# Squares in tiles of their own, x loaded once, weight loads in another order: a two-layer streaming encoder on 8 cores

## The reference

```
xn   = rms_norm(x, norm_mix)                       # x * rsqrt(mean(x*x) + eps) * g
q, k, v, pin, gates = split(xn @ w_in)             # 512, 128, 128, 512, 2 x 1024
q, k = rms_norm per head
a    = sliding-window attention(q, k, v) with ALiBi and a sink logit in the denominator
pl   = (trailing means of pin over 2, 4, 8, 16 frames - pin) @ w_pool * pool_scale
mix  = sigmoid(gates_0) * (a @ w_br_attn) + sigmoid(gates_1) * (pl @ w_br_pool)
x    = x + mix @ w_out
h    = rms_norm(x, norm_ffn) @ w_up                # 1024 -> 2 x 2816
hc   = conv_b + causal depthwise conv of width 3 over h
x    = x + (gelu(hc_gate) * hc_val) @ w_down       # 2816 -> 1024
```

## Time and profile before

| what | value |
|---|---|
| runs | 3413.95, 3782.05 and 3413.5 us, median 3413.95 |
| the profiled execution | 3412.9 us, of which the span of core 2 is 3411.3 |
| spans of cores 0 to 7 | 3407.0, 3378.5, 3411.3, 3379.6, 3380.1, 3408.5, 3407.7, 3378.3 |
| busy: PE, DVE, ACT, POOL | 3300.8 (97%), 2138.6 (63%), 1563.4 (46%), 990.5 (29%) |
| chain that ended last | PE 89%, DMA 5%, DVE 2%, issue 2%, ACT 1% |
| DMA | 385.28 MB, mean 113 GB/s |
| layer 0 mixer, FFN; layer 1 mixer, FFN | 0 to about 800, to 1760, to 2490, to 3411 us |

### The profile page before, as it was taken

The page is one execution under the profiler, slowest core; times in us unless marked ns, Lnnn a source line. Parts: engine busy times, 40 slices in busy tenths (PEclk is TensorE's granted clock), DMA queues, the critical chain, the costliest instruction groups (busy, mean ns, idle before and its releaser), DMA issues.

```text
span 3411.3 us, 53613 instructions; the slowest of 8 cores (3378.3 to 3411.3 us)
## 1 busy us (share of the span) xinstructions
PE 3300.8 (97%) x17682; PEld 1613.6 (47%) x17835; DVE 2138.6 (63%) x3379; ACT 1563.4 (46%) x2417; POOL 990.5 (29%) x1057
## 2 busy tenths in 40 slices
PE   6899999999999999999988899999989999999999
PEld 3544444444444444444444444444445555555554
DVE  3555556646667766677645455656476666776666
ACT  3444444425444644455535344444254444554444
POOL 3233322114323433234333222221143222333222
PEclk8899999999999999999988999999999999999999
DMA  9356666456523344233562333332543221212211
GB/s 194 82 159 139 145 140 139 103 170 213 148 82 95 90 130 118 82 96 94 174 209 57 101 99 99 100 99 77 176 173 108 89 79 56 77 56 89 88 45 45
DMA packets 186640, 385.28 MB, mean 113 GB/s; under 512 B 31712, under 2 KB 110208, under 8 KB 179648
## 3 DMA queue, kind: packets, MB, share of 16 engines
q1 hardware_dynamic: 173296, 279.43, 26.3%
q0 software_dynamic: 6592, 56.79, 10.4%
q10 hardware_dynamic: 6480, 45.62, 3.8%
HBM read 369.01 MB, written 115.41 MB: 142 GB/s over the span
## 4 chain that ended last, share of the span: by engine, by line
PE 89%; DMA 5%; DVE 2%; issue 2%; ACT 1%; POOL 0%; SPq 0%; ACTq 0%; DVEq 0%; POOLq 0%
PE psb L615 89%; DMA xsl<-xT 2%; DMA xsl<-x 1%; DMA xst<-xT 1%; DVE xn L624 1%; ACT psb L618 0%; PE psb L1117 0%; DVE PT L621 0%; ACT srt L618 0%; DMA xm<-xsl 0%; DMA w_kv<-wun 0%; DMA x<-xsl 0%; ACT L618 0%; DVE xsl L624 0%; DMA xst<-x0p 0%
## 5 line engine op out<-in xcount | busy, mean ns | idle before, releaser
L615 PE MATMUL psb<-xn,w_up 128*128 128x482 bf16 (+3 forms) x6336 | 1264.0, 362 | 16.4 <-DVE xsl L624 16.4
L615 PEld LDWEIGHTS psb<-xn,w_up 128*128 128x128 bf16 x6336 | 620.4, 98 | 657.0 <-issue 24.7
L621 POOL TENSOR_TENSOR actT<-ug,uv 128x480 bf16<-128x480 f32 (+3 forms) x360 | 424.7, 1180 | 1135.6 <-ACT ug L618 987.5
L624 DVE SCALAR_TENSOR_TENSOR ug<-psb,pv,ug 128x480 f32<-128x480 f32 (+3 forms) x792 | 557.5, 704 | 125.7 <-ACT ug L618 42.5
L615 PE MATMUL psb<-actT,w_dn 128*128 128x480 bf16 (+3 forms) x3168 | 631.3, 361 | 0.0
L624 DVE SCALAR_TENSOR_TENSOR uv<-psb,pv,uv 128x480 f32<-128x480 f32 (+3 forms) x792 | 557.2, 703 | 51.9 <-ACT uv L618 4.6
L618 ACT ACTIVATE ug<-psb,pv 128x480 f32<-128x480 f32 (+3 forms) x396 | 291.9, 737 | 558.1 <-PE psb L615 545.1
L615 PE MATMUL psb<-xn,w_eg 128*128 128x512 bf16 x1970 | 473.5, 380 | 3.7 <-issue 0.3
L615 PEld LDWEIGHTS psb<-actT,w_dn 128*128 128x128 bf16 x3168 | 310.0, 98 | 315.5
L618 ACT ACTIVATE uv<-psb,pv 128x480 f32<-128x480 f32 (+3 forms) x396 | 292.7, 739 | 224.0 <-PE psb L615 223.4
L618 ACT ACTIVATE tg<-psb,hgb 128x512 f32<-128x512 f32 (+2 forms) x288 | 185.1, 649 | 306.9 <-PE psb L615 286.5
(11 more groups left out here) (165 smaller groups left out, 2685.6 us busy)
## 6 DMA issues: line engine op xcount, KB each, us to landing
xsl<-x SPq DMA_DIRECT2D x96, 512.0 KB, 4.8
xsl<-xT SPq DMA_DIRECT2D x88, 512.0 KB, 6.0
wb<-wun POOLq DMA_DIRECT2D x42, 1024.0 KB, 11.0
xm<-xsl SPq DMA_DIRECT2D x64, 512.0 KB, 5.2
xsl<-xm SPq DMA_DIRECT2D x56, 482.0 KB, 7.8
xsl<-xm SPq DMA_DIRECT2D x56, 460.0 KB, 4.4
w_up<-wb ACTq DMA_DIRECT2D x22, 1024.0 KB, 7.4
xsl<-xm SPq DMA_DIRECT2D x28, 480.0 KB, 4.9
```

What stands on the lines that cost most here:

```text
L615: S.op("pe", lambda e: e.matmul(out=out, lhsT=lhsT, rhs=rhs, start=start, stop=stop), reads=reads, writes=writes)
L621: S.op(eng, lambda e: e.tensor_tensor(out=out, in0=a, in1=b, op=op), reads=reads, writes=writes)
L624: S.op("dve", lambda e: e.scalar_tensor_tensor(out=out, in0=a, scalar=s, in1=b, op0=op0, op1=op1), reads=reads, writes=writes)
```

## The change

1. `sqx0` to `sqx2`, three tiles of [128, 512] fp32, take the squares, one block of 128 channels at a time. The sum runs in `sqx0` on POOL; the squares alternate between `sqx1` and `sqx2`. x stays in its slot until `scale`, and the second `loads()` goes, except for the norm of layer 1's third group (in `ffn_down` of layer 0's last group).
2. up6 to up10 move into the first FFN group, after pairs j = 0, 2, 4, 6, 8, and dn0 to dn5 follow after j = 10, 12, ..., 20.
3. Layer 1's small group has its residual in `resS`, loaded at the start of the layer.
4. For groups 1 and 2 of each layer the pooling difference reads `pinb` and not the bank, and the bank is given back before the window sums.
5. The second group's x at the start is loaded right behind `pv` and no longer waits for `w_kv`; `w_kv` no longer waits for `xst0_1`.
6. The planner: DMAs of different queues share the rate (280 bytes per ns), a 64-row matmul of 256 columns or more costs 0.76 of a full one and not 0.5.
7. The tile `spare` goes; `xst0` lies over `padE`, `resS`, `padF` and `mixT`.

```diff
-DMA_START, DMA_END, DMA_RATE = 1400, 600, 300.0
+DMA_START, DMA_END, DMA_RATE = 1400, 600, 280.0
...
-        return c / 2 if p.ins[0].shape[0] == 64 and n >= 256 else c
+        return c * 0.76 if p.ins[0].shape[0] == 64 and n >= 256 else c
...
+        def serve(queue, t, size):
+            t = max(t + DMA_START, busy.get(queue, 0.0))
+            ends = sorted(u for q, u in busy.items() if q != queue and u > t)
+            left = float(size)
+            while ends and t + left * (1 + len(ends)) / DMA_RATE > ends[0]:
+                left -= (ends[0] - t) * DMA_RATE / (1 + len(ends))
+                t = ends.pop(0)
+            busy[queue] = t + left * (1 + len(ends)) / DMA_RATE
+            return busy[queue] + DMA_END
...
+        sqx = [sb(f"sqx{i}", [128, 512], F32) for i in range(3)]
...
+        resS = su("m", "resS", [128, KT, 18], F32, rows("resS", 4, 144))
...
             def stat(self, p):
                 A, B = self.A, self.B
-                if self.keep is not None:
...
-                i = self.slot[p]
-                act(xs[i][:, :, A:B], xs[i][:, :, A:B], ACTF.Square, [f"xs{i}"], [f"xs{i}"])
-                if p > 0:
-                    a = self.acc
-                    tt("pool", xs[i][:, :, A:B], xs[a][:, :, A:B], xs[i][:, :, A:B], ALU.add, [f"xs{a}", f"xs{i}"], [f"xs{i}"])
-                self.acc = i
+                for h in range(2):
+                    k = 2 * p + h
+                    if self.keep is not None:
+                        X, xr, b = self.keep[0][:, k, A:B], f"{self.keep[1]}{p}", k % 3
+                    else:
+                        i = self.slot[p]
+                        X, xr, b = xs[i][:, h, A:B], f"xs{i}", 0 if k == 0 else 1 + k % 2
+                    if self.keep is not None and self.keep[2] is not None and h == 1:
+                        tt("dve", sqx[b][:, A:B], X, X, ALU.mult, [xr], [f"sqx{b}"])
+                    else:
+                        act(sqx[b][:, A:B], X, ACTF.Square, [xr], [f"sqx{b}"])
+                    if self.keep is None:
+                        if k > 0:
+                            tt("pool", sqx[0][:, A:B], sqx[0][:, A:B], sqx[b][:, A:B], ALU.add, ["sqx0", f"sqx{b}"], ["sqx0"])
+                        continue
+                    if k == 0:
+                        self.bk = PB.get()
+                    mm(psb[:, self.bk, A:B], onesf[:, :], sqx[b][:, A:B], k == 0, k == KT - 1, ["onesf", f"sqx{b}"], pr(self.bk))
...
+            if G.i < 3 and G.samp is None:
+                PB.put(bk)
             window(G, j, r, n, G.C0, bk, 0 if G.own else G.C0)
...
-            stt(G.eD[0][:, j, col + c0:col + n], cur[:, 16 + c0:16 + n], 1.0 / w, psb[:, bk, b0 + c0:b0 + n], ALU.mult, ALU.subtract,
-                [cr] + pr(bk), [dr])
+            stt(G.eD[0][:, j, col + c0:col + n], cur[:, 16 + c0:16 + n], 1.0 / w, pinb[r][:, 16 + c0:16 + n] if flat else psb[:, bk, b0 + c0:b0 + n], ALU.mult, ALU.subtract,
+                [cr] + ([f"pinb{r}"] if flat else pr(bk)), [dr])
...
+                    if own:
+                        stt(resS[:, 2 * p + hh, :], psb[:, bks[c], C0:N], 0.5, resS[:, 2 * p + hh, :], ALU.mult, ALU.add,
+                            pr(bks[c]) + [f"resS{p}"], [f"resS{p}"])
...
         nj0.loads()
         dma(pv[:], pvec, [], ["pv"], "c0")
+        nj1.loads()
...
-        load_first("kv", ["xst0_1"])
+        load_first("kv")
         load_first("pin")
         load_first("q")
-        for p in range(4):
-            nj1.load(p, ["w_kv"])
...
         nj2.stat_end()
-        nj2.loads()
...
                         if m == 5:
                             job.stat_end()
-                        if m == 6:
-                            job.loads()
...
-                if nxt is None:
-                    load_w(l, "up6", "up7")
...
-                if nxt is None:
-                    load_w(l, "up8", "up9", "up10")
...
-                    if i == 0 and j % 2 == 0 and j < 12:
-                        load_w(l, f"dn{j // 2}")
+                    if i == 0 and j % 2 == 0 and j < 10:
+                        load_w(l, f"up{6 + j // 2}")
+                    if i == 0 and j % 2 == 0 and j >= 10:
+                        load_w(l, f"dn{j // 2 - 5}")
...
                 ffn_up(l, g, mid)
-                if job is not None:
-                    job.loads()
```

## The result

| | before | changed |
|---|---|---|
| median | 3416.59 us | 3370.61 us |
| ratio to before, 95% interval | | 0.9858 (0.9846 to 0.9870) |
| same kernel in a second series | 3412.28 us | 3363.27 us, 0.9854 (0.9838 to 0.9870) |
| profiled execution | 3412.9 us | 3370.6 us |

The account below looks back on a forecast made before the run. TensorE, busy 97% of the span, was taken as the bound, with only its idle and slow stretches to shorten. 3412.9 - 20 (boundaries) - 12 (start) - 10 (layer switch) = 3370.9, predicted 3371 us, range 3340 to 3406.

Parts of the forecast that it names:

- Boundaries: The two changes from mixer to FFN: spreading the weight loads gives back 20 us of 10.8 + 10.9 lost on core 2.
- The reading by the lag between two cores of a die: Core 2's lag behind core 1 at the same weight loads: 10.8 us at boundary 1, 10.9 at boundary 2.
- The rival with the pair: At the boundaries the cores of a pair hinder each other whatever is loaded, so no gain there: 3391 us, chance 0.10.
- Start: Start of layer 0: earlier second-group x 5 us, bank given back early 4, x reload and low clock 3, together 12.
- 27.4 + 10.5 + 3 for the root gives 41 where the second group started at 50.0: Start: first group's pin matmuls end, plus 16 matmuls of squares, plus root; second group 9 us earlier.
- Planner: New planner costs in the whole kernel only reorder instructions: 0 us, bounds -3 and +10.
- Bank early: Pooling difference reads the copy in pinb, so its bank is free before it: 4 us at the start, 1 at the switch.
- Layer switch: From 1740 to 1960 us: residual tile 6, third group's norm 3, pooling difference 1, together 10 us, bounds -18 and +2.
- the residual's tile: Layer switch: the small group's residual, loaded long before in its own tile, saves 6 of 7.3 us of waits.
- x once: 33 norm jobs no longer reload 2 MB each, some 65 MB of 385; 0 us inside mixer and FFN.
- Lock: Shared SBUF port: 16 two-SBUF-operand pooling differences, taken as 0; the rival had 16.8 us, 3388, chance 0.05.
- Slower by ACT waiting for POOL: All 33 norm jobs: squares wait for POOL's adds in two alternating tiles, 84 us lost, 3455 us, chance 0.09.

## Why the prediction was right, step by step

**Boundaries: right.** Taken 20 us; 20 alone, 19 when undone, 10.7 and 9.8 by the marks of the slowest core. The reading by the lag between two cores of a die gave both the place and the size. The rival with the pair, by which the loads don't matter, is refuted by the loads alone (20 us). That the two cores of a pair also hinder each other while there is a burst fits the marks before and with the loads undone, but is not shown.

**Start: size right (12 taken, 10.4 measured on the slowest cores, 10 to 15 in the means of the two executions), composition wrong.** The prediction had the second group's keys near 43 us. The lines of core 6 say, for the first, second and third group:

```profile
29.35 0.49 PE L626 MATMUL psb<-xn,w_kv 128*128 128x400 bf16 x1 [11.98 <-DVE xn L635]
...
52.50 0.39 PE L626 MATMUL psb<-w_kv,xn 128*128 128x128 bf16 x4 [2.81 <-DVE xn L635]
...
93.35 0.59 PE L626 MATMUL psb<-xn,w_kv 128*128 128x512 bf16 x1 [1.67 <-DVE xn L635]
```

and before, second and third:

```profile
48.28 0.38 PE L615 MATMUL psb<-xn,w_kv 128*128 128x512 bf16 x1 [2.76 <-DVE xn L624]
...
103.03 0.59 PE L615 MATMUL psb<-xn,w_kv 128*128 128x512 bf16 x1 [2.50 <-DVE xn L624]
```

The second group is 4.2 us later than before, and the whole gain, 9.7 us, is there by the third. The failed step is "27.4 + 10.5 + 3 for the root gives 41 where the second group started at 50.0": it took the first group's end as it was before and left ACT's queue out. On that queue stands, in the changed kernel:

```profile
20.05 0.55 ACT L629 ACTIVATE psb<-psb,epst 128x400 f32<-128x400 f32 x1
27.34 0.63 ACT L629 ACTIVATE sqx<-xst 128x512 f32<-128x512 f32 x1 [6.74 <-DMA xst<-xT]
27.88 0.49 ACT L629 ACTIVATE psb<-psb 128x400 f32<-128x400 f32 x1
```

The logarithm of the first group's root ends at 20.6, and its exponential, behind a square of the second group's x that waits for its load until 27.3, starts at 27.9. The planner sorts by its own simulated times, and placed that square ahead of the exponential. The prediction had 4 us for loads that share the engines with x0p; the first keys came 12.0 us late (29.4 against 17.4 on core 6 before). The rest of the sum can be followed on core 6:

```profile
39.55 3.95 PE L626 MATMUL psb<-xn,w_pin 128*128 128x226 bf16 x32
...
43.33 6.19 PE L626 MATMUL psb<-sqx,onesf 128*128 128x512 f32 x14
```

The first group's pin matmuls end near 43.4 and not at 27.4, the 14 sums of squares that are left then take 6.2 us, and the root 3 more: 52.5. The x loads themselves did come earlier, if not by 30: the last piece landed at 35.7 us, against 42.3 before, and its square starts only at 47.0. So x no longer was what the second group waited for. TensorE's waits in the first 150 us show the late first keys as well; the first line has one of 12.0 us:

```profile
PE psb L626 <- DVE xn L635: 17.3, 5, 12.0
```

The waits on dT are out of that window's list (4.9 us in the earlier trace rows).

**Planner: wrong.** The prediction took 0 and argued that a full stretch can't gain. That holds for the full stretches (939 and 998 us in the table with either set of costs) and says nothing of the start, where the new costs gave 14 to 20 us, against 6 to 7 lost at the switch: 15 us in sum by the ratio. The bounds of -3 and +10 missed it on the side of gain.

**Bank early: too small.** 5 taken, 15 in the changed kernel, 5 alone. The sum priced 4.9 us of waits on dT at the start; that the 5 us alone come from there is not shown, since the marks have 1 us of it in the first stretch.

**Layer switch: size right (10 taken, 11.3 and on the mean 12 to 13 measured), composition wrong again.** The sum gave 6 us to the residual's tile, which gives 2 to 3, and 1 to the bank, which gives 7 to 8. The new planner takes 6 to 7 back. It gave 3 to the third group's norm, partly since "its scaling needs no second load"; that was a misreading of the change, which leaves the second load of layer 1's third group where it was. These parts, each undone by itself, come to less than half of the 12 to 13 us, so the rest is open; the tiles of the squares are the part that no run undid. TensorE's waits from 1690 to 1960 us on core 6:

```profile
PE psb L626 <- DVE PT L632: 6.8, 5, 3.5
...
PE psb L626 <- DVE resS L635: 1.8, 1, 1.8
```

The largest is the chain of PT that the prediction named as next. The wait on resS, 1.8 us once, is above the 1 us that the prediction allowed; on cores 0, 2 and 4 it is 0.7 or less.

**x once: right** at 0 in the body. **Lock: right** to take near 0, by the 2.3 us read above, on an engine that is not the bound. The rival's 16.8 us was also too high a price by its own row: it counted 16 whole durations of 1.05 us, of which some 0.68 each were there before. **Slower by ACT waiting for POOL:** the body's stretches are those of the cores that had no gap before (939 us and 998 us), so nothing of it reached TensorE.

So the boundaries, 20 of the 42 us, were forecast by their cause; that the rest came out as well was luck. Errors of both signs met: planner and bank were worth 25 us more than forecast by undoing them one at a time, and the tile 3 or 4 less. The six parts undone one by one give 19, 2 to 19, 15, 15, 2 and 4 us, some 66 with the middle of the open one, where all together give 49. With the intervals of six ratios this difference is not clear of noise; that parts need each other is seen best in the bank, with 15 us beside the rest and 5 alone.

## What to carry to other kernels

Where several cores run one program, compare the marks of two cores: a lag that grows at one place prices that place, and at the two boundaries here the price was good to about 1 us (10.8 and 10.9 read, 10.7 and 9.8 gained). Spread a burst of loads over the work that needs it later, above all beside a load that is needed at once. In a stretch full of gaps the order on in-order queues is worth as much as any wait that can be read off, so a change of a planner's costs can't be taken as 0 there; and an instruction that waits for a load should not stand ahead of a chain that is ready.

## What the runs showed of the hardware that was not expected

- Issuing a load can hold its queue for long, and in the two orders tried here it went by where the load stood and not by its size. In the changed kernel hvt (0.5 KB), behind x0p and the second group's x and beside the casting loads on POOL's queue, took 9.20 us to issue on SP, and sph 3.30 (lines above). With the small loads ahead of that x, hvt took 0.53 us and the four loads of x 12.33 together, in order of time on core 6:

```profile
3.54 0.53 SPq L642 DMA_DIRECT2D hvt<-hv  x1
...
6.91 12.33 SPq L642 DMA_DIRECT2D xst<-xT  x4
```

- Holding 14 MB of casting loads on POOL's queue back until the second group's x had landed (issue of w_brp at 35.5 and not at 22.1 us) moved the whole by 18 us, 0.9907 against 0.9854, with the same bytes and each run's own order of instructions.
- A DVE operation with two SBUF inputs that ran beside one of POOL took up to 1.64 us and not 0.67, and one of 16 columns up to 1.15 and not 0.17. Such long ones are few: over the 24 operations the sum rose by 2.3 us.
